# A two-block layer on one core: where the masks of the delta rule's inverse are applied

## The reference, cut to what matters

```python
k_beta = k * beta[..., None]
lower = jnp.where(strict, jnp.einsum('bhncd,bhnmd->bhncm', k_beta, k) * decay, 0.0)
t_inv = lax.linalg.triangular_solve(lower, eye, left_side=True, lower=True, unit_diagonal=True)
u = jnp.einsum('bhncm,bhnme->bhnce', t_inv, v * beta[..., None])
w = jnp.einsum('bhncm,bhnmd->bhncd', t_inv, k_beta * jnp.exp(g_cum)[..., None])
```

## Time and profile before

| what | value |
|---|---|
| time, median of 3 runs | 2920.41 us (2914.79 to 2922.92) |
| profiled execution | 2919.66 us |
| its span in the trace | 2918.0 us |
| PE busy | 2601.9 us, 89% of the span |
| DVE busy | 1124.4 us, 39% |
| ACT busy | 827.4 us, 28% |
| POOL busy | 250.3 us, 9% |
| mean granted clock of PE | 0.946 |

### The profile page before, as it was taken

The page is one execution under the profiler, slowest core; times in us unless marked ns, Lnnn a source line. Parts: engine busy times, 40 slices in busy tenths (PEclk is TensorE's granted clock), DMA queues, the critical chain, the costliest instruction groups (busy, mean ns, idle before and its releaser), DMA issues.

```text
span 2918.0 us, 30014 instructions
## 1 busy us (share of the span) xinstructions
PE 2601.9 (89%) x12308; PEld 1940.4 (66%) x12308; DVE 1124.4 (39%) x1537; ACT 827.4 (28%) x1317; POOL 250.3 (9%) x240
## 2 busy tenths in 40 slices
PE   6898989999998999969999959786999959999996
PEld 4787878787776777758778757564687744443442
DVE  4656555434442323343334351536433461111113
ACT  5434434232232223232233232423532200000000
POOL 0213131302110000000000000322000000000000
PEclk9999999999999999979999979898999969999998
DMA  4122121222222333212222133110213267999995
GB/s 152 43 66 73 51 73 59 87 91 70 100 101 103 128 117 114 94 58 87 87 87 87 65 138 117 53 64 15 93 63 130 74 245 295 409 409 409 409 409 223
DMA packets 155278, 404.68 MB, mean 139 GB/s; under 512 B 7440, under 2 KB 25232, under 8 KB 155024
## 3 DMA queue, kind: packets, MB, share of 16 engines
q1 hardware_dynamic: 150032, 385.04, 35.4%
q0 software_dynamic: 5120, 17.83, 1.8%
HBM read 387.91 MB, written 14.94 MB: 138 GB/s over the span
## 4 chain that ended last, share of the span: by engine, by line
PE 80%; DVE 7%; ACT 4%; DMA 4%; issue 2%; POOL 1%; SPq 0%; DVEq 0%; POOLq 0%; ACTq 0%
PE banks L93 17%; PE banks L95 17%; PE banks L94 17%; PE banks L1761 5%; PE banks L1792 4%; PE banks L1742 2%; PE banks L1819 2%; PE banks L1649 2%; PE banks L1624 2%; DMA work<-w_down_in 1%; DMA ring<-w_down_in 1%; PE banks L1348 1%; PE banks L1345 1%; DVE ring_split L87 1%; PE banks L1441 1%
## 5 line engine op out<-in xcount | busy, mean ns | idle before, releaser
L93 PE MATMUL banks<-work_split,ring_split 128*128 128x512 f32 (+1 forms) x1568 | 629.4, 401 | 48.9 <-DVE ring_split L87 26.0
L87 DVE TENSOR_TENSOR ring_split<-ring,ring_split 128x1024 fp32r<-128x1024 f32 (+1 forms) x292 | 356.0, 1237 | 787.1 <-ACT ring_split L82 787.1
L94 PE MATMUL banks<-work_split,ring_split 128*128 128x512 f32 (+1 forms) x1568 | 613.9, 392 | 0.0
L95 PE MATMUL banks<-activations_T_split,ring_split 128*128 128x512 f32 x1184 | 467.9, 395 | 0.0
L82 ACT ACTIVATE ring_split<-ring 128x1024 fp32r<-128x1024 f32 (+1 forms) x292 | 299.9, 1045 | 334.9 <-PE banks L95 260.6
L93 PEld LDWEIGHTS banks<-work_split,ring_split 128*128 128x128 f32 x1568 | 299.6, 191 | 114.5 <-DVE ring_split L87 30.3
L94 PEld LDWEIGHTS banks<-work_split,ring_split 128*128 128x128 f32 x1568 | 299.8, 191 | 59.8 <-issue 1.0
L94 PE MATMUL banks<-ring_split,work_split 128*128 128x512 f32 (+1 forms) x752 | 294.3, 391 | 0.0
L95 PE MATMUL banks<-ring_split,work_split 128*128 128x512 f32 (+1 forms) x752 | 293.8, 391 | 0.0
L95 PEld LDWEIGHTS banks<-activations_T_split,ring_split 128*128 128x128 f32 x1184 | 225.7, 191 | 49.1
L93 PE MATMUL banks<-ring_split,work_split 128*128 128x512 f32 x400 | 159.4, 398 | 15.1 <-DVE ring_split L87 10.0
(11 more groups left out here) (288 smaller groups left out, 3201.4 us busy)
## 6 DMA issues: line engine op xcount, KB each, us to landing
ring<-w_gate_up_in SPq DMA_DIRECT2D x32, 2048.0 KB, 23.8
ring<-w_in_in SPq DMA_DIRECT2D x31, 2048.0 KB, 7.8
ring<-w_down_in SPq DMA_DIRECT2D x24, 2048.0 KB, 15.7
work<-w_gate_up_in SPq DMA_DIRECT2D x24, 2048.0 KB, 24.5
work<-w_down_in SPq DMA_DIRECT2D x12, 2048.0 KB, 18.1
ring<-w_in_in SPq DMA_DIRECT2D x17, 1024.0 KB, 7.7
ring<-w_up_in SPq DMA_DIRECT2D x8, 2048.0 KB, 8.2
activations_T<-w_gate_up_in SPq DMA_DIRECT2D x8, 2048.0 KB, 23.6
```

What stands on the lines that cost most here:

```text
L87: s.mark(dve.tensor_tensor(R(dst), src, R(hi).bitcast(F32), ALU.subtract), what)
L93: pe.matmul(out, R(ll), R(rh), start=start, stop=False)
L94: pe.matmul(out, R(lh), R(rh), start=False, stop=False)
L95: return pe.matmul(out, R(lh), R(rl), start=False, stop=stop)
```

## The change

POOL's masks of levels 1 to 6 go (the one of level 0 stays), and so do ACT's copies. PE multiplies the unmasked tile `LT` by X. DVE reads the product from PSUM bank A, multiplies it by the level's mask and writes `PP`. The result is the same because X is block-diagonal at every level: a block of `L X` is a block of L times one diagonal block of X, so the mask may be applied before or behind the product. As it now lies on P rather than on the transposed tile, the masks of levels 1 to 6 are transposed.

```diff
@@ POOL, chain_a
-                for s in range(LEVELS):
-                    for j in range(2):
-                        if s == 0:
-                            pool.wait_ge(*c_vec(f"LT{j}.{p}"))
-                            if p:
-                                pool.wait_ge(*c_pe(f"P{LEVELS - 1}_{j}.{p - 1}"))
-                        else:
-                            pool.wait_ge(*c_pe(f"P{s - 1}_{j}.{p}"))
-                        if s == 1:
-                            pool.wait_ge(*c_vec(f"Y0_{j}.{p}"))
-                        c_pool.mark(pool.tensor_tensor(by_t(NM[:, j, :]), LT[j], m_lvl[:, s, :].unsqueeze(1).broadcast_to([P, NT, P]), ALU.mult),
-                                    f"NM{s}_{j}.{p}")
+                for j in range(2):
+                    pool.wait_ge(*c_vec(f"LT{j}.{p}"))
+                    if p:
+                        pool.wait_ge(*c_pe(f"P0_{j}.{p - 1}"))
+                    c_pool.mark(pool.tensor_tensor(by_t(NM[:, j, :]), LT[j], m_lvl[:, 0, :].unsqueeze(1).broadcast_to([P, NT, P]), ALU.mult),
+                                f"NM0_{j}.{p}")
@@ ACT, chain_a
                 for s in range(1, LEVELS):
-                    for j in range(2):
-                        act.wait_ge(*c_pe(f"P{s}_{j}.{p}"))
-                        if s > 1:
-                            act.wait_ge(*c_pe(f"Y{s - 1}_{j}.{p}"))
-                        elif p:
-                            act.wait_ge(*oa_st[j](f"o.{p - 1}"))
-                        c_act.mark(act.activation(PP[j], by_t(bank_a[j][:, :]), ACT.Copy), f"P{s}_{j}.{p}")
                     fill(sum(FILL["level"]))
@@ PE, chain_a
                 for s in range(1, LEVELS):
                     for j in range(2):
-                        pe.wait_ge(*c_pool(f"NM{s}_{j}.{p}"))
                         pe.wait_ge(*c_vec(f"X{s - 1}_{j}.{p}"))
                         for t, c in enumerate(c4):
-                            mm = pe.matmul(bank_a[j][:, c], NM[:, j, c], X[j][:, t, :], start=True, stop=True)
+                            mm = pe.matmul(bank_a[j][:, c], LT[j][:, t, :], X[j][:, t, :], start=True, stop=True)
                         c_pe.mark(mm, f"P{s}_{j}.{p}")
                     fill(FILL["level"][0])
                     for j in range(2):
-                        pe.wait_ge(*c_act(f"P{s}_{j}.{p}"))
+                        pe.wait_ge(*c_vec(f"P{s}_{j}.{p}"))
@@ DVE, chain_a
                 for s in range(1, LEVELS):
                     for j in range(2):
+                        dve.wait_ge(*c_pe(f"P{s}_{j}.{p}"))
+                        if s > 1:
+                            dve.wait_ge(*c_pe(f"Y{s - 1}_{j}.{p}"))
+                        c_vec.mark(dve.tensor_tensor(PP[j], by_t(bank_a[j][:, :]), m_lvl[:, s, :].unsqueeze(1).broadcast_to([P, NT, P]), ALU.mult),
+                                   f"P{s}_{j}.{p}")
+                    for j in range(2):
@@ constants
-        lv.append(-(same & (i[:, None] // w % 2 == 0) & (i[None, :] // w % 2 == 1)).astype(float))
+        upper = -(same & (i[:, None] // w % 2 == 0) & (i[None, :] // w % 2 == 1)).astype(float)
+        lv.append(upper.T if s else upper)
```

## The result

| | before | after |
|---|---|---|
| median, 7 runs of each | 2919.82 us (2913.70 to 2922.92) | 2930.47 us (2926.58 to 2933.31) |
| profiled execution | 2919.66 us, span 2918.0 | 2933.31 us, span 2931.5 |

The ratio after to before is 1.0043, with a 95% interval of 1.0032 to 1.0054: 0.43% slower, clear of the 0.3%. The median rose by 10.65 us. The forecast was 2936.5 us, 16.1 over the median of the three runs then known, with a range of 2925 to 2945. Every ratio in this document compares fast executions with fast ones; two executions of the last experiment, of 3170.90 and 11460.17 us, were slow and are left out.

What follows compares the result with a forecast made beforehand. PE was taken to bound the levels. 2919.66 us plus 11.0 for DVE's queue and 5.2 for three clock falls gave 2935.9, as a median 2936.5 us; the 8-in-10 range was 2925 to 2945.

Steps and rivals of the forecast that it cites:

- What bounds the levels: Levels of each pair: PE is busy 62.33 of 63 us in pair 0; at most 0.67 us a pair winnable.
- worth nothing by themselves: Levels 1 to 6: the 48 masks leaving POOL released no PE wait, so removing them gains nothing directly.
- The queue: Levels 1, 4, 5 of pairs 0 to 2: masks behind DVE's older work delay PE 3.66 us a pair, 11.0 in all.
- The short form of DVE's work: DVE's convolutions in the levels: 2.32 us for three instructions once POOL is idle, against 3.34 beside its masks.
- The queue does not bite: Levels: masks land before PE wants them; 2920.4 us less at most 2.9; chance 0.16, including biting in part.
- faster: Levels: ACT's late copies and POOL's interference go, no mask comes late; 2917.5 us; chance 0.04.
- Dearer: Levels 1, 4, 5: DVE's stretches stay long though POOL is idle; 26 us plus clock falls, 2956 us; chance 0.06.
- the long form: DVE's slower convolutions in the levels, 3.34 us beside POOL's masks, kept as the upper end.
- a further wait for X of the level before: Levels: PE waits for X instead, so masks stay on the chain; time stays at 2920; no separate chance given.
- The clock: Behind six new PE waits in levels 1 and 5: 0 to 10.3 us from clock falls, 5.2 taken.
- What ACT's copies cost: Levels 1 and 5 of pairs 0 to 2: late copies cost 0.96 us a pair, 2.9 us at most.

Runs made afterwards that it cites:

- the last experiment: 1.8 us of double PE work in pair 0, added to the changed kernel with masks ahead of DVE's other work (0.9981 against before) and to the changed kernel (1.0048).
- the shifted kernel: Changed kernel with the wT products done twice in pair 0, 1.8 us more PE work; 2930.19 us, ratio 1.0048 against the kernel before.

## Why the prediction was right or wrong

**What bounds the levels** was right: PE does, and others' work counts only by lateness. Taking POOL's masks alone away moved nothing (0.9996), as "worth nothing by themselves" said.

**The queue** was right in its place and its size, and this was worked out, not luck. Levels 1, 4 and 5 of pairs 0 to 2 were predicted late, levels 2, 3 and 6 and pair 3 not, and the trace agrees in each. The four times from P worked out for pair 0 are met within 0.02 us. Putting the masks ahead of the queue, with nothing else changed, took the loss away, which shows the cause rather than argues it. 11.0 us were predicted for it; the three pairs' levels are 3.81, 3.73 and 3.93 us longer, 11.5 together. In pair 0 levels 1, 4 and 5, from one P to the next, are longer by 1.78, 0.74 and 1.29 us, where 1.76, 0.62 and 1.28 were predicted.

**The short form of DVE's work** was right: all convolutions at 2.32 us without POOL. The other end of that range is shown too: with POOL's masks left in place the convolution took 3.33 us, the wait was 3.42 us and the loss 35 us.

**The rivals.** "The queue does not bite" and "faster" are excluded by the result. "Dearer" put the long form down to ACT, PE and the transfers; the kernel without POOL's masks shows that POOL was its cause (3.34 to 2.32 us). Where POOL's masks were kept, the rival's restart of PE in level 1 of pair 0 came true to 0.01 us. No sign of a further wait for X of the level before appeared.

**The clock** was the mis-sized term. 5.2 us were put on three falls behind the new waits, taken as the middle of none and six from two rows of a later stage. None of the six waits of 1.88 us had a fall behind it, in the profiled execution, nor had the six of the shifted kernel; this term measures 0. Without it the forecast is 11.0 us over before; the medians differ by 10.65. So what failed is the step from a wait's length in another stage to a fall in this one. It was not for want of rows: the trace of before has two more waits of that length with the clock at 1.00 ahead of them, at 1941.71 (1.93 us) and 2099.16 (1.92 us), and the clock fell behind both (PE's granted clock is the third number from the end):

```profile
1941.70:1945.70 4.00, 3.99 (x22) 4.00 (x23) 1.76 (x3) 0.78 (x2) 0.00 (x0) 0.63 1.04 394
...
2099.10:2103.10 4.00, 3.94 (x10) 3.15 (x11) 3.41 (x4) 2.03 (x2) 0.00 (x0) 0.58 0.92 314
```

So did it behind the three waits of 2.56 us at the ends of pairs 0 to 2, in the very stage. All five, had they been counted, would have moved the term toward its upper bound of 10.3 us, away from the 0 measured; that the forecast is not 5 us farther off is luck. Why a wait of 1.92 us has a fall behind it there and one of 1.88 us has none here, no run shows. A length alone does not decide: two equal waits of 2.62 us ended differently, and behind the wait of 1.93 us the clock is 1.00 in the trace after (1958.1 to 1962.1 us).

**What ACT's copies cost.** The ceiling, 0.96 us a pair, was also a little low: with no waits at all the levels are 1.4 us a pair shorter than before, 1.27 of it in levels 1 and 5. The delay counted from P to PE's restart misses 0.15 us of each of the two. This did not touch the forecast, which counts from where PE restarted before.

## What to carry to other kernels

Work moved to another engine, however idle that one is on average, is priced by its place in that engine's queue: add up what stands in front of it in the order, from the time when the first of that is released, and compare with the time at which the waiting engine runs out of cover. If it comes late, the cure is the order on the receiving engine or more cover on the waiting one; either turned this change from 0.43% slower to 0.4% faster (0.9961, 0.9964) than the kernel before, and the cover alone gave the kernel before 0.2%. A part of each gain, 3.4 to 5.1 us in the profiled executions, is falls of the clock that happened to be missing. Before crediting a change with a gain, give the old kernel the same cure.

## What the runs showed of the hardware

- POOL's SBUF multiplications slow DVE's with two SBUF inputs: three of them 3.34 us beside POOL, 2.32 without, 4.26 at worst; no single instruction of a convolution took over 755 ns once POOL's masks were gone, where the longest had been 1784. In the trace of before line 1932, which reads two SBUF tiles, took 1.46 to 1.48 us beside them and at most 0.69 otherwise; line 1936, which reads PSUM and one SBUF tile, took 0.68 to 0.69 all eight times beside them. The extra costs nothing until DVE's queue is on PE's path, and then it is more than half of the loss (8.65 us a pair by the sums against 3.66, and 35 us in all against 11).
- In the levels of the traces here the clock fell behind none of twelve waits of 1.86 to 1.89 us, behind none of three of 2.4, one of two of 2.62, and all ten of 3.3 us and over. In later stages of before it fell behind three waits of 1.92 and 1.93 us. Each fall costs about 1.7 us (16.38 against 14.67 us for the same work). The same wait of 2.56 us at the end of a pair had a fall behind it in 17 of 30 cases in ten traces, three of three in some kernels and none in others, and work of 1.8 us ahead of it changed which. Gains or losses of a few microseconds in this kernel can be such falls and not the edit.
